# A one-core hybrid decoder step: memory chunks used one by one, x tiles turned into six banks at full height, both weight tiles per row chunk in the first up unit

## The reference, cut to what matters

```python
mn = rmsnorm(mem, g_mem); mem_k, mem_v = mn @ w_mem_k, mn @ w_mem_v      # 256 memory rows
xn = rmsnorm(x, g_pre_mix); proj = xn @ w_in
a, b, c = rwkv7_mix(...), sgu_mix(...), mem_xattn(...)
mix = (sum over n of sigmoid(gates[n]) * (branch[n] @ w_branch[n])) @ w_out
h = x + rmsnorm(mix, g_post_mix)
up = rmsnorm(h, g_pre_ffn) @ w_up                                        # 2048 x 11264
f = (gelu(gate) * val) @ w_down, with (gate, val) the causal 3-tap convolution of up
y = h + rmsnorm(f, g_post_ffn)
```

## Time and profile before

| | us |
|---|---|
| median of 3 runs (lowest, highest) | 2447.63 (2447.49, 2448.1) |
| the profiled execution: its time, its span | 2445.91, 2444.2 |
| busy in the span: PE, PEld, DVE, ACT, POOL | 2392.5, 2273.3, 1467.3, 893.4, 121.0 |
| mean granted PE clock | 0.995 of full |

### The profile page before, as it was taken

How to read it: one execution, slowest core, us unless ns; L and a number is a source line. 1 busy time by engine, 2 the same in 40 slices (tenths; PEclk the granted TensorE clock), 3 DMA queues, 4 the chain that set the end, 5 groups by cost and what they waited for, 6 DMA issues and landing times.

```text
span 2444.2 us, 48594 instructions
## 1 busy us (share of the span) xinstructions
PE 2392.5 (98%) x19598; PEld 2273.3 (93%) x19598; DVE 1467.3 (60%) x2060; ACT 893.4 (37%) x1038; POOL 121.0 (5%) x195
## 2 busy tenths in 40 slices
PE   8999999999999999999999998999999999999998
PEld 6799888899888888888999987999999999999998
DVE  5545544565677666776545446666665666666676
ACT  6343344343333233332434333333333333333334
POOL 2000010100000010000000001000000000000003
PEclk9999999999999999999999998999999999999999
DMA  7554376343332243322444632444444444444443
GB/s 261 175 167 143 127 282 243 126 135 97 99 94 81 94 140 99 94 80 93 143 154 145 205 120 86 143 151 149 149 148 150 149 147 154 137 154 154 150 143 109
DMA packets 282189, 346.67 MB, mean 142 GB/s; under 512 B 6957, under 2 KB 240733, under 8 KB 280907
## 3 DMA queue, kind: packets, MB, share of 16 engines
q1 hardware_dynamic: 272315, 308.44, 38.7%
q0 software_dynamic: 9712, 36.30, 4.5%
q10 hardware_dynamic: 32, 0.01, 0.0%
HBM read 333.83 MB, written 10.89 MB: 141 GB/s over the span
## 4 chain that ended last, share of the span: by engine, by line
PE 86%; DVE 8%; issue 3%; DMA 1%; ACT 1%; DVEq 0%; SPq 0%; POOL 0%; ACTq 0%
PE bank L248 20%; PE bank L257 20%; PE bank L249 19%; PE bank L227 5%; PE bank L228 5%; PE bank L229 5%; PE bank L1152 5%; DVE work L893 1%; ACT hi L211 1%; DVE lo L218 1%; PE bank L1168 1%; DVE q L820 1%; PE bank L477 1%; PE bank L1626 1%; DMA raw<-in_w_out 0%
## 5 line engine op out<-in xcount | busy, mean ns | idle before, releaser
L248 PE MATMUL bank<-ah,hi 128*128 128x320 f32 x3232 | 970.9, 314 | 7.8 <-DVE al L1943 7.2
L218 DVE TENSOR_TENSOR lo<-raw,hi 128x2048 fp32r<-128x2048 f32 x286 | 655.8, 2293 | 519.5 <-ACT hi L211 503.1
L249 PE MATMUL bank<-al,hi 128*128 128x320 f32 x3232 | 957.5, 310 | 0.0
L211 ACT ACTIVATE hi<-raw 128x2048 fp32r<-128x2048 f32 x286 | 547.9, 1916 | 943.7 <-PE bank L257 691.7
L248 PEld LDWEIGHTS bank<-ah,hi 128*128 128x128 f32 x3232 | 608.7, 188 | 24.4 <-issue 18.2
L249 PEld LDWEIGHTS bank<-al,hi 128*128 128x128 f32 x3232 | 609.2, 188 | 0.3
L257 PE MATMUL bank<-ah,lo 128*128 128x320 f32 x3232 | 554.3, 312 | 0.0
L257 PEld LDWEIGHTS bank<-ah,lo 128*128 128x128 f32 x3232 | 492.3, 188 | 5.1 <-issue 1.6
L227 PE MATMUL bank<-bh,hi 128*128 128x320 f32 x704 | 219.0, 311 | 0.2 <-DVE work L2214 0.2
L228 PE MATMUL bank<-bl,hi 128*128 128x320 f32 x704 | 217.9, 309 | 0.0
L229 PE MATMUL bank<-bh,lo 128*128 128x320 f32 x704 | 217.8, 309 | 0.0
(11 more groups left out here) (361 smaller groups left out, 2000.8 us busy)
## 6 DMA issues: line engine op xcount, KB each, us to landing
raw<-in_w_in SPq DMA_DIRECT2D x98, 1024.0 KB, 5.2
raw<-in_w_up SPq DMA_DIRECT2D x88, 1024.0 KB, 5.1
raw<-in_w_down SPq DMA_DIRECT2D x44, 1024.0 KB, 5.1
raw<-in_w_branch SPq DMA_DIRECT2D x24, 1024.0 KB, 5.4
raw<-in_w_out SPq DMA_DIRECT2D x16, 1024.0 KB, 5.5
raw<-in_w_mem_k SPq DMA_DIRECT2D x8, 1024.0 KB, 5.6
raw<-in_w_mem_v SPq DMA_DIRECT2D x8, 1024.0 KB, 5.2
work<-in_cache_mem_k POOLq DMA_DIRECT2D x8, 1024.0 KB, 6.3
```

The costliest lines, as they stand in the source:

```text
L211: act.activation(hi[c % NS][:, :], raw[c % 2][:, :], ACT.Copy).then_inc(S("hi_done"), 1)
L218: dve.tensor_tensor(lo[c % NS][:, :], raw[c % 2][:, :], hi[c % NS][:, :], ALU.subtract)\
L248: pe.matmul(out, w, xh[:, 8 * h + k, :], start=h + k == 0, stop=False)
L249: pe.matmul(out, w, xl[:, 8 * h + k, :], start=False, stop=False)
```

## The change

1. Entry: `entry_pe` turns only k = 0 and 1. ACT's order is mem_hi 0, 1, hi_unit 0, 1, mem_hi 2, 3; DVE's is gain 0, 1, mem_lo 0, 1, lo_unit 0, gain 2, 3, mem_lo 2, 3, lo_unit 1. In `mem_pe` k = 2, 3 are turned between the halves of unit 0, k = 4, 5 at its end, k = 6, 7 between the halves of unit 1. In every unit of the stage PE waits for `hi_done`, makes the eight products of a half with `hi`, waits for `lo_done` (first half), and makes the four with `lo`.
2. The sample's tile of x is turned at full height: its partitions 64 to 127 are cleared by POOL (`x_pad`, in `qr` at the start, in `rwr` ahead of the x loads of the residual stage), and all three transposes are 128 x 128.
3. Residual stage: the turned x tiles go to banks 4, 5, 6, 7, 2, 3 (`x_bank`), six ahead; `lo_unit(155)` stands behind the fourth lo part of `hn` and not ahead of the second root.
4. First up group: `first_up_pe` waits for a chunk, uses it for both tiles c, and makes the `lo` products of both tiles at the end of each unit.

```diff
@@ -240,9 +240,7 @@
                     for k in range(8):
-                        if chunks == "hn_lo" and c == 0 and k % 2 == 0:
-                            pe.wait_ge(S(chunks), 4 * h + k // 2 + 1)
-                        elif chunks and chunks != "hn_lo" and c == 0 and k % 4 == 0:
+                        if chunks and c == 0 and k % 4 == 0:
                             pe.wait_ge(S(chunks), 2 * h + k // 4 + 1)
@@ -274,6 +272,7 @@
         x_tok = [wk[:, 896:896 + D], wk[:, 896 + D:896 + 2 * D], qr[0:TS, 0:D]]
+        x_turn = x_tok[0:2] + [qr[:, 0:D]]
         mem_tok = [rwr[:, 0:D], rwr[:, D:2 * D]]
@@ -335,6 +334,7 @@
             keep(rep8.rearrange("p (b t) -> p b t", b=8), ALU.not_equal, 0, [[0, 8], [-1, 8]], 1, 1.0, "consts")
+            pp.do(pool.memset(qr[TS:P, 0:D], 0.0), "x_pad")
@@ -392,11 +392,11 @@
             mem_hi_part(act, aa, 0)
+            mem_hi_part(act, aa, 1)
             hi_unit(act, 0)
-            mem_hi_part(act, aa, 1)
+            hi_unit(act, 1)
             mem_hi_part(act, aa, 2)
             mem_hi_part(act, aa, 3)
-            hi_unit(act, 1)
@@ -414,11 +414,12 @@
             vv.do(dve.memset(ss, 1.0), "rs_zero")
-            for k in range(3):
-                mem_gain(dve, vv, k)
+            mem_gain(dve, vv, 0)
+            mem_gain(dve, vv, 1)
             mem_lo_part(dve, vv, 0)
+            mem_lo_part(dve, vv, 1)
             lo_unit(dve, 0)
-            mem_lo_part(dve, vv, 1)
+            mem_gain(dve, vv, 2)
             mem_gain(dve, vv, 3)
@@ -444,8 +445,8 @@
             pe.transpose(bank[7][:, 496:512], gm_row, ident[0:KD, 0:KD]).then_inc(S("gm_ps"), 1)
-            for k in range(4):
-                mem_turned(pe, k)
+            mem_turned(pe, 0)
+            mem_turned(pe, 1)
@@ -473,8 +474,7 @@
             for t in range(3):
-                m = TS if t == 2 else P
-                last = pe.transpose(out[:, 128 * t:128 * t + m], toks[t][:, 128 * k:128 * k + 128], ident[0:m, 0:m])
+                last = pe.transpose(out[:, 128 * t:128 * t + 128], toks[t][:, 128 * k:128 * k + 128], ident[:, :])
             return last
@@ -488,26 +488,38 @@
                             pe.wait_ge(S("tok_normed"), 3)
+                            pe.wait_ge(S("x_pad"), 1)
                             pe.wait_ge(S("prm_ready"), 1)
-                        x_transposes(pe, x_tok, k, bank[4 + k % 4]).then_inc(S("entry_ps"), 1)
-                pe.wait_ge(S("lo_done"), u + 1)
+                        x_transposes(pe, x_turn, k, bank[4 + k % 4]).then_inc(S("entry_ps"), 1)
+                pe.wait_ge(S("hi_done"), u + 1)
                 for tt in range(2):
...
                     if tt and u < 2:
-                        mem_turned(pe, 4 + 2 * u)
-                        mem_turned(pe, 5 + 2 * u)
+                        mem_turned(pe, 2 + 4 * u)
+                        mem_turned(pe, 3 + 4 * u)
                     if tt and u == 6:
                         parameters_pe(pe)
+                    r = slice(128 * tt, 128 * tt + 128)
+
                     for k in range(4):
-                        kk, r = 4 * (u % 4) + k, slice(128 * tt, 128 * tt + 128)
+                        kk = 4 * (u % 4) + k
                         if u < 4 and tt == 0 and k % 2 == 0:
                             pe.wait_ge(S("mem_lo"), kk // 2 + 1)
-                        a_h, a_l = ah[:, kk, r], al_[:, kk, r]
-                        w_h, w_l = hi[s][:, 512 * k:512 * k + 512], lo[s][:, 512 * k:512 * k + 512]
-                        last = three(pe, bank[t % 4][:, :], a_h, a_l, w_h, w_l, kk == 0, kk == KD - 1)
+                        w = hi[s][:, 512 * k:512 * k + 512]
+                        pe.matmul(bank[t % 4][:, :], ah[:, kk, r], w, start=kk == 0, stop=False)
+                        pe.matmul(bank[t % 4][:, :], al_[:, kk, r], w, start=False, stop=False)
+
+                    if tt == 0:
+                        pe.wait_ge(S("lo_done"), u + 1)
+                    for k in range(4):
+                        kk = 4 * (u % 4) + k
+                        last = pe.matmul(bank[t % 4][:, :], ah[:, kk, r], lo[s][:, 512 * k:512 * k + 512], start=False, stop=kk == KD - 1)
                     last.then_inc(S("parts"), 1)
+                if u == 0:
+                    mem_turned(pe, 4)
+                    mem_turned(pe, 5)
             pe.wait_ge(S("consts"), 1)
@@ -1882,12 +1894,14 @@
         x2_tok = [rwr[:, 0:D], rwr[:, D:2 * D], rwr[0:TS, 2 * D:3 * D]]
+        x2_turn = x2_tok[0:2] + [rwr[:, 2 * D:3 * D]]
         cst_raw = qr[:, 0:11 * P]
...
             pool.wait_ge(S("bl_ready"), 2)
+            pp.do(pool.memset(rwr[TS:P, 2 * D:3 * D], 0.0), "x_pad")
             for k in range(2):
@@ -1934,8 +1948,7 @@
                 dve.wait_ge(S("res_ps"), k + 1)
-                vv.do(dve.tensor_tensor(mix[:, k, :], mo[:, k, :], bank[4 + k % 4][:, 0:T], ALU.add), "h_ready")
-            lo_unit(dve, U_FFN + 1)
+                vv.do(dve.tensor_tensor(mix[:, k, :], mo[:, k, :], x_bank(k)[:, 0:T], ALU.add), "h_ready")
             rms_root_dve(dve, vv, 1)
@@ -1949,21 +1962,27 @@
                     lo_parts(c - 1)
+                if c == 4:
+                    lo_unit(dve, U_FFN + 1)
             lo_parts(7)
+
+        def x_bank(k):
+            return bank[(4, 5, 6, 7, 2, 3)[k % 6]]
...
             pe.wait_ge(S("x2_in"), 64)
-            for k in range(4):
-                x_transposes(pe, x2_tok, k, bank[4 + k]).then_inc(S("res_ps"), 1)
+            pe.wait_ge(S("x_pad"), 2)
+            for k in range(6):
+                x_transposes(pe, x2_turn, k, x_bank(k)).then_inc(S("res_ps"), 1)
                 if k == 0:
...
             for k in range(KD):
-                if k + 4 < KD:
+                if k + 6 < KD:
                     pe.wait_ge(S("h_ready"), k + 1)
-                    x_transposes(pe, x2_tok, k + 4, bank[4 + k % 4]).then_inc(S("res_ps"), 1)
+                    x_transposes(pe, x2_turn, k + 6, x_bank(k)).then_inc(S("res_ps"), 1)
                 pe.wait_ge(S("h_squared"), k + 1)
@@ -1983,9 +2002,32 @@
-        def up_pe(pe, u, t, k=0, i=0, chunks=None):
+        def first_up_pe(pe, u, t):
+            for c in range(2):
+                bank_free(pe, t + c)
+            for h in range(2):
+                pe.wait_ge(S("hi_done"), u + h + 1)
+                s = (u + h) % NS
+                for k in range(8):
+                    if k % 2 == 0:
+                        pe.wait_ge(S("hn_lo"), 4 * h + k // 2 + 1)
+                    for c in range(2):
+                        w = hi[s][:, 256 * k + 128 * c:256 * k + 128 * c + P]
+                        pe.matmul(bank[(t + c) % 4][:, 0:T], w, ah[:, 8 * h + k, :], start=h + k == 0, stop=False)
+                        pe.matmul(bank[(t + c) % 4][:, 0:T], w, al_[:, 8 * h + k, :], start=False, stop=False)
+                pe.wait_ge(S("lo_done"), u + h + 1)
+                for c in range(2):
+                    for k in range(8):
+                        w = lo[s][:, 256 * k + 128 * c:256 * k + 128 * c + P]
+                        last = pe.matmul(bank[(t + c) % 4][:, 0:T], w, ah[:, 8 * h + k, :], start=False, stop=h + k == 8)
+                    last.then_inc(S("parts"), 1)
+
+        def up_pe(pe, u, t, k=0, i=0, first=False):
             for g in range(2):
-                pe_group(pe, u + 2 * g, t + 2 * g, ah, al_, 2, 12 if k else 0, 24 if k else 0, i, None if g else chunks)
+                if first and g == 0:
+                    first_up_pe(pe, u, t)
+                else:
+                    pe_group(pe, u + 2 * g, t + 2 * g, ah, al_, 2, 12 if k else 0, 24 if k else 0, i)
@@ -2008,7 +2050,7 @@
         def ffn_pe(pe):
-            up_pe(pe, UF, TF, 0, 0, "hn_lo")
+            up_pe(pe, UF, TF, 0, 0, True)
             up_pe(pe, UF + 4, TF + 4)
```

## The result

| | before | after |
|---|---|---|
| median (lowest, highest), runs | 2447.63 (2444.86, 2451.51), 5 | 2435.23 (2433.95, 2437.73), 5 |
| the profiled execution: its time, its span | 2445.91, 2444.2 | 2437.73, 2436.0 |
| mean granted PE clock of that execution | 0.995 | 0.993 |

The ratio is 0.995, with a 95% interval from 0.9935 to 0.9964: faster by 12.4 us in the medians. The two profiled executions differ by only 8.2 us; the one after was the slowest of its five.

A forecast was written before the change was run, and what follows sets the result against it. PE, busy 98%, was taken as the bound, with time won only in its waits, half clock or spacing. Terms 1.0 + 4.0 + 4.1 + 1.6 = 10.7 us gave a median of 2436.9 us, range 2432.8 to 2442.0.

The forecast's parts named there:

- the forecast case: Whole kernel: all four edits gain, 10.7 us in sum, median 2436.9 us; chance 0.67.
- Entry: 0 to 56 us: PE starts 4.3 us earlier but waits for parameters in unit 6; 1.0 us kept, bounds 0.3 and 3.0.
- Units 8 to 15: Memory stage's x transposes: full-height sample tiles remove idle time around 64-row loads; 4.0 us, bounds 0 and 4.6.
- The rival that the padding does nothing: Sample transposes: loads of 64 and 128 rows take equal time; 3.6 us left in all, 2444.0; chance 0.08.
- Residual stage: Sum-of-squares loop: cheaper rounds and six banks, with 6 us at half clock; 4.1 us, bounds 1.0 and 6.1.
- The rival of full clock in this loop: Residual loop: PE never falls to half clock; 1.9 us more gain, 2435.0; chance 0.12.
- First up group: Both weight tiles used per chunk; group ends 22.4 us after first hn, not 24.0; 1.6 us, bounds 0 and 2.0.
- The slower rival: Up units: half clock holds on through this group and the next; 18.0 us lost against 10.7 won, 2454.9; chance 0.03.
- The second memset: POOL, ahead of the residual stage's x loads: those were issued 100 us before their use, so no effect.
- Stages between are bound by PE ... and pass the gain on: Stages between the edited stretches: PE sets their pace relative to its own progress, so earlier gains carry through.

The follow-up runs named there:

- all three edits: Changed kernel plus spatial-gating products filled to 128 rows, parameter loads issued one unit earlier, and lo_unit(155) ahead of the second root: 2423.39 us, ratio 0.9898.
- full height in the gating: Changed kernel with the spatial gating's one-row bias and 64-row sample products filled with zeros to 128 rows: 2426.29 us, ratio 0.9912.
- the kernel with both edits: Changed kernel with lo_unit(155) back ahead of the second root and the parameter loads issued one unit earlier: 2428.99 us, ratio 0.9925.

## Why the prediction was right

The median of 2435.23 lies 1.7 below the 2436.9 forecast, in the range, and the forecast case, not one of its rivals, is what the traces show. Step by step:

- **Entry**, forecast 1.0, measured 2.6 between the two profiles, 0.5 in the second profile of the changed kernel, 1.6 between the medians of ten. The mechanism held: the gain is what hi_unit(5), load 7 and the parameters gain, and PE waits for them (1.42 and 1.65 us, forecast 1 to 2). What the prediction took as fixed is when the clock rises. In the first profile it rises during the eight hi products, lo_unit(1) ends at 21.09 and hi_unit(4) and (5) come 2.9 and 2.7 us earlier. In the second, as in six of the ten profiles with the new entry, all eight run at half clock as counted: lo_unit(1) ends at 22.90, in the forecast 22.3 to 22.9, and hi_unit(5) is 0.7 us earlier. The 1.0 is near for such an execution and too small for the others.
- **Units 8 to 15**, forecast 4.0, measured 4.6, the upper bound: six transposes take 0.57 us where 0.60 was taken, and the step from 64 rows back to 128, read as free, costs 0.07 each time. The rival that the padding does nothing is refuted by undoing it. The spacing of the earlier trace rows decided, not the duration of a load. The Trainium skill's rule ("TensorE: Matmul & The Clock Gate", LDWEIGHTS (loading the stationary operand)) holds for the durations, 136 against 139 ns; taken as a bound on the cost it fails here by 0.52 us for six transposes of which two had 64 rows.
- **Residual stage**, forecast 4.1, measured 5.2. The sum on record has a slip: 1457.4 and 14.9 make 1472.3 and not 1472.7, so that its own terms give 4.5. Rounds are as forecast; the half clock lasted 3.4 us, where 6 had been taken over from before. This length is no property of the kernel either: of the nine profiles with six banks and full height eight have 3.4 us, and that of all three edits has 6.8 (T to R 24.5). The rival of full clock in this loop was half right.
- **First up group**, forecast 1.6, measured 1.7: R+22.4 as worked out, while the R+24.0 of before was read at the start of the last product and is R+24.2 at its like, with waits of 0.54 to 0.60 for the chunks behind lo_unit. The slower rival, half clock holding on, did not come: the clock was full from 1481.68 on. The remark that lo_unit(155) ahead of the root saves some 2 us more was right (2.2).
- **The second memset**, forecast nothing, measured up to 0.9. It was costed by what it delays, the x loads of the residual stage, and not by what those loads delay. The twelve profiles with the memset gain 0.6 (two of them, the changed kernel's first one too) to 0.9 us between 1340 and 1450. The padding undone and the padding alone are among them, both with 0.9, and have only the memsets in common; one was not tried by itself.
- **"Stages between are bound by PE ... and pass the gain on"** is the step that failed in the profiled execution: bound by PE they are, but PE's own clock fell there. The terms as measured in it are 2.6 + 4.6 + 0.6 + 5.2 + 1.7 = 14.7, less 6.0 at half clock and 0.4 in small pieces: the 8.2 of the spans, but for rounding. The prediction rests on no row between unit 15 and the residual stage.

The sum of 10.7 came near the 12.4 of the medians in part by luck: terms that were too small stood against a loss that was not in it. That loss is no constant: 13.7 us of half clock in one execution of the changed kernel, 3.4 in another. The kernel before had none near 268 us in its profile, but its runs at a granted clock of 0.991 to 0.993 show that it pays for more half clock in some executions too, so that part of the loss falls away between medians; how much is not known.

Left open: why the same kernel has 3.4 us of half clock in one execution and 13.7 in another. With full height in the gating it is absent in both profiles, without full height in two of eleven. That the low products are a condition of it is likely, not proved, and they are not enough for it: the kernel with both edits has them and none of it. Where the stage starts doesn't decide either, as far as these profiles go: its first product lies at 263.54 with 13.7 us of half clock and at 263.89 with none. The removed gaps and the greater height came together and were not told apart.

## What to carry to other kernels

In a stream of short products each change of height between two stationary operands cost idle time, in both directions (0.17 us from 128 rows to 64 and 0.07 back, 0.44 from one row to 128), and none stood between two of the same low height. Where zeros can be put under the low ones once, filling them is cheap (a memset of 1.8 us on POOL here), and such places are to be sought in every stage, not only where the waits are. Where PE is busy 100%, read the granted clock beside it: busy time hides both gaps and half clock. Put a piece of another engine's work where that engine pauses, not in the middle of the chunks that feed PE.

## What the runs showed of the hardware

- TensorE fell to half clock (1.2 GHz) with no idle time in its row (5.00 us busy of 5.00), in a stretch of products of 1, 64 and 128 rows; the same work at full height kept 2.4 GHz in both profiles that had it. Each us of half clock cost 0.44.
- A weight load of 64 rows took 136 ns and one of 128 rows 139 to 140, but where the height changed between two loads, idle time of 0.07 to 0.44 us stood before the second.
- At the entry the granted clock rose to 1.00 between 3.0 and 6.0 us after the first weight product in the ten profiles with the new entry (first product at 10.84 to 11.73), and between 4.0 and 5.7 us after it in the three with the old (15.48 to 15.53).
- In the residual stage PE was idle for 2.5 to 4.3 us, and about the end of that the clock fell, for 3.4, 6.8 or 10.2 us: 3.4 in nine of the eleven profiles with full-height transposes and 6.8 in two, 6.8 and 10.2 in the two with 64 rows.
